# Turning the softmax weights of the hybrid layers with VectorE blocks and DMAs

## The chip, the cores and the metric

The kernel runs on one NeuronCore of a Trainium2 chip. The metric is the device time of one execution in microseconds (us), the median over several runs. Its five engines each work through a queue of their own, in order: PE (TensorE, the matrix products), DVE (VectorE), ACT (ScalarE), POOL (GpSimd) and SP (SyncE, which here issues every DMA). An instruction that must wait for a semaphore holds up all that stands behind it in its queue.

## The reference

Input is one sequence of 512 tokens, 1024 wide, in float32. One first block runs, then two hybrid layers, then a final norm. The change is in the hybrid layers, whose part that matters here is this:

```
def hybrid_layer(x, norm_gain, w_in, w_out, rel_bias, cos, sin):
    hn = rms_norm_2(x, norm_gain)
    proj = hn @ w_in                       # 1024 -> 4096
    aq, ak, av, ag, rq, rk, rv, rg = split(proj, 8 parts of 512)
    ya = chunked_rel_attention(aq, ak, av, rel_bias)   # 8 heads of 64
    yr = chunkwise_retention(rq, rk, rv, cos, sin)     # 4 heads of 128
    y = concatenate([ya * silu(ag), yr * silu(rg)])
    return x + y @ w_out
# chunked_rel_attention, one head, chunks of 64, 8 chunks to the left visible:
    scores = q k^T * dh**-0.5 + bias[distance]         # only keys up to the query's own chunk
    p = softmax(scores)
    out = p v
```

With 512 tokens every query sees all keys up to the end of its own chunk, so a head's softmax weights are the lower triangle of a 512x512 matrix, in blocks of 128.

## The kernel before, in words

All products are made in three parts of fp32r: high half times high half, and the two mixed ones. A stream of weight tiles feeds them: W.load() issues the DMA of a tile into one of NRAW raw buffers (line 277), W.split() makes its high half on ACT (line 290) and one step later its low half on DVE (line 292), and issues the load of the tile NRAW further on (line 295). Four high and four low buffers (NW) hold the split tiles. One product of a tile is 24 matmuls of 512 columns.

The order of all side work is written by hand. Each eight such matmuls count as one step (hook, line 216). A piece of side work is a Python generator: `yield n` puts its rest n steps later. So side work is spread over the product stream in fixed slots, on whichever engine it needs, in program order.

In a hybrid layer, layer_b(l), eight attention heads (head(i), line 1223) start six steps apart (line 1446), head 0 at step 13 or 12. Counted from a head's start, these are its slots in the kernel before: 0, scores of three query blocks (PE). 1, bias and row minimum (DVE). 2, last score (PE), exponentials (ACT). 3, bias of the last (DVE), load of a later head's bias (SP). 4, last exponential. 5, reciprocal (DVE) and four scalings of p (ACT, line 1274). 7, eight PE transposes into banks 5 and 6 (turn, line 1278). 8, high halves (ACT). 9, low halves (DVE). 10 to 12, the same for the two transposes that are left. 13, eight matmuls with the values (line 1305), then the copy and add to YB. Head 0 of the first hybrid layer has one step less before its transposes. The heads overlap: a head's slot 13 is the next head's slot 7. In this text AV(i) is the matmuls of head i with the values, score(i) its first scores.

Keys are made by ev_k (line 1124): they are scaled, and double_k (line 632) writes each half of 64 partitions twice, in its own place and in the other half, in high and low parts: four ACT and four DVE instructions of 64x512. After the eight heads come four retention heads, ret(i), and the output product.

The lines that the change touches otherwise: the start of the kernel, where spread_a (line 847) turns the first norm into rows and makes the FOLD matrix with six DVE instructions before the first projections are evacuated, and the placing of the buffers (lines 78 to 128).

## Time and profile before

| | us |
|---|---|
| median of 3 runs | 1222.63 (1222.36 to 1224.81) |
| the profiled execution, its own time | 1224.13 |
| span of its trace | 1222.3 |
| PE busy | 1208.9 (99%) |
| DVE busy | 842.9 (69%) |
| ACT busy | 589.4 (48%) |
| POOL busy | 287.8 (24%) |

Busy time of an engine is the time in which one of its instructions runs. The granted clock of PE is 0.8 of 2.4 GHz in the first slice of the page, and 0.9 or more in all others. Times in rows below are us from the start of the span unless they are marked ns.

### The profile page before, as it was taken

How to read it: one execution, taken by the hardware profiler on the slowest of the kernel's cores; microseconds unless marked ns; L12 is line 12 of the kernel's file. 1: busy time of each engine (PE TensorE's matmuls, PEld its weight loads, DVE VectorE, ACT ScalarE, POOL GpSimd, SP SyncE). 2: the span in 40 equal slices, each digit the busy share in tenths (PEclk: the TensorE clock that was granted, in tenths of full speed). 3: DMA queues.
4: the chain of work that ended last, by engine and by line, in shares of the span. 5: the costliest groups of instructions: out<-in, count | busy, mean ns of one | idle time of the engine just before them, and what ended most of it. 6: DMA issues, size and time to landing. Idle time of an engine off the chain costs nothing.

```text
span 1222.3 us, 15898 instructions
## 1 busy us (share of the span) xinstructions
PE 1208.9 (99%) x6061; PEld 1027.0 (84%) x6061; DVE 842.9 (69%) x1361; ACT 589.4 (48%) x1080; POOL 287.8 (24%) x299
## 2 busy tenths in 40 slices
PE   8999999999999999999999999999999999999998
PEld 7788888888888888888888879899888889899886
DVE  5889655556776577537758887767747686766746
ACT  6666432333433334224336477664435577654442
POOL 0220499912000000000006761111414211212300
PEclk8999999999999999999999999999999999999999
DMA  7422333233423433233324332222214332222211
GB/s 218 124 83 64 101 87 103 88 102 95 130 78 90 126 96 94 86 108 100 103 70 131 90 99 88 79 85 71 69 52 138 109 91 87 78 69 71 77 45 69
DMA packets 196032, 114.35 MB, mean 94 GB/s; under 512 B 3994, under 2 KB 190836, under 8 KB 195828
## 3 DMA queue, kind: packets, MB, share of 16 engines
q1 hardware_dynamic: 195956, 113.35, 31.5%
q8 instruction: 47, 0.77, 0.3%
q14 instruction: 29, 0.24, 0.1%
HBM read 111.23 MB, written 2.10 MB: 93 GB/s over the span
## 4 chain that ended last, share of the span: by engine, by line
PE 95%; DVE 3%; ACT 1%; issue 1%; DMA 1%; SPq 0%; DVEq 0%; ACTq 0%
PE ps L190 92%; PE ps L193 3%; DVE b_sets L163 1%; DMA xtm<-in_x_dram 1%; DVE wlo L163 0%; ACT b_p L160 0%; ACT whi L160 0%; DVE fold L163 0%; ACT x1l L160 0%; DVE b_pt L163 0%; DVE tmp L163 0%; DVE b_s L166 0%; SPq L196 0%; DVE nrm L166 0%; DVE b_sets L166 0%
## 5 line engine op out<-in xcount | busy, mean ns | idle before, releaser
L160 ACT ACTIVATE whi<-raw 128x1024 fp32r<-128x1024 f32 (+1 forms) x198 | 206.6, 1051 | 294.1 <-PE ps L190 293.7
L163 DVE TENSOR_TENSOR wlo<-raw,whi 128x1024 fp32r<-128x1024 f32 (+1 forms) x192 | 245.4, 1285 | 50.5 <-ACT whi L160 49.8
L190 PE MATMUL ps<-x0l,whi 128*128 128x512 f32 x1008 | 257.6, 394 | 0.0
L190 PE MATMUL ps<-x0h,whi 128*128 128x512 f32 x1008 | 255.4, 391 | 0.0
L190 PE MATMUL ps<-x0h,wlo 128*128 128x512 f32 x1008 | 254.3, 390 | 0.0
L190 PEld LDWEIGHTS ps<-x0h,whi 128*128 128x128 f32 x1008 | 188.0, 188 | 38.1
L190 PEld LDWEIGHTS ps<-x0h,wlo 128*128 128x128 f32 x1008 | 187.8, 188 | 38.3
L190 PEld LDWEIGHTS ps<-x0l,whi 128*128 128x128 f32 x1008 | 186.5, 188 | 37.4
L163 POOL TENSOR_TENSOR sums<-sums,sq 128x512 f32<-128x512 f32 x28 | 43.2, 1555 | 423.6 <-ACT sq L160 423.6
L190 PE MATMUL ps<-x1h,wlo 128*128 128x512 f32 x304 | 82.3, 389 | 0.0
L190 PE MATMUL ps<-x1h,whi 128*128 128x512 f32 x304 | 82.3, 389 | 0.0
L190 PE MATMUL ps<-x1l,whi 128*128 128x512 f32 x304 | 82.2, 389 | 0.0
L163 DVE TENSOR_TENSOR tmp<-ps,rb 128x512 f32<-128x512 f32 x54 | 37.0, 687 | 52.9 <-PE ps L190 52.7
L166 DVE SCALAR_TENSOR_TENSOR h<-ps,h 128x512 f32<-128x512 f32 x40 | 27.4, 688 | 65.2 <-PE ps L190 65.2
L160 ACT ACTIVATE b_p<-b_p,smx 128x512 f32<-128x512 f32 (+3 forms) x128 | 65.9, 553 | 8.1 <-DVE smx L177 5.2
L190 PEld LDWEIGHTS ps<-x1h,whi 128*128 128x128 f32 x304 | 57.0, 188 | 11.9
L190 PEld LDWEIGHTS ps<-x1l,whi 128*128 128x128 f32 x304 | 57.1, 188 | 11.8
L190 PEld LDWEIGHTS ps<-x1h,wlo 128*128 128x128 f32 x304 | 57.0, 188 | 11.8
L166 DVE SCALAR_TENSOR_TENSOR f_c<-f_u,cols,f_c 128x512 f32<-128x512 f32 x88 | 65.8, 749 | 1.6
L163 DVE TENSOR_TENSOR f_u<-ps,rb 128x512 f32<-128x512 f32 x44 | 30.3, 691 | 52.4 <-PE ps L190 52.3
L163 DVE TENSOR_TENSOR b_sets<-tmp,b_sets 64x512 fp32r<-64x512 f32 (+1 forms) x64 | 49.1, 768 | 15.1 <-ACT b_sets L160 13.8
L160 ACT ACTIVATE b_sets<-tmp 64x512 fp32r<-64x512 f32 (+1 forms) x64 | 40.2, 628 | 36.9 <-POOL tmp L163 34.9
(187 smaller groups left out, 1705.6 us busy)
## 6 DMA issues: line engine op xcount, KB each, us to landing
raw<-in_w_in_dram SPq DMA_DIRECT2D x98, 512.0 KB, 4.0
raw<-in_w_up_dram SPq DMA_DIRECT2D x44, 512.0 KB, 3.8
raw<-in_w_out_dram SPq DMA_DIRECT2D x24, 512.0 KB, 3.6
raw<-in_w_down_dram SPq DMA_DIRECT2D x16, 512.0 KB, 3.6
b_m<-in_rel_bias_dram SPq DMA_DIRECT2D x16, 256.0 KB, 3.3
raw<-in_w_down_dram SPq DMA_DIRECT2D x8, 384.0 KB, 3.1
xtm<-in_x_dram SPq DMA_DIRECT2D x4, 512.0 KB, 7.5
raw<-in_w_attn_branch_dram SPq DMA_DIRECT2D x8, 256.0 KB, 2.9
```

What stands on the lines that cost most here:

```text
L160: return AC.put(lambda e: e.activation(o, i, func, **kw), after, AC, 1)
L163: return on.put(lambda e: e.tensor_tensor(o, a, b, op), after, on, 1)
L166: return DV.put(lambda e: e.scalar_tensor_tensor(o, a, s, b, op0, op1), after, DV, 1)
L190: return PE.put(lambda e: e.matmul(o, l, r, start=start, stop=stop), after, PE if mark else None, 1)
L193: return PE.put(lambda e: e.transpose(o, i, ident), after, PE if mark else None, 1)
```

## The change

For each of the 16 heads (eight in each hybrid layer) the ten PE transposes go. In their slot, 7, DVE turns the weights in 32x32 blocks (six instructions, 1280 columns in all) into a buffer PD, and SP issues 16 DMAs of 32 partitions x 320 floats (40 KB each) that put the blocks in their places in PX; they wait for the last DVE instruction. In slot 10 ACT makes the high half of all 1280 columns in one instruction, which waits for all 16 DMAs. In slot 11 DVE makes the low half in one. AV stays in slot 13, but its moving operand and its output are now four pieces each, one for each 32 queries of a block, of 128, 96, 64 or 32 columns; the add to YB puts the order right.

For each of the four key tiles of a layer, double_k_by_dma makes the own half alone (two ACT and two DVE instructions), and four DMAs of 64 partitions x 512 floats (128 KB each) copy it into the other half. The DMA of the high parts waits for ACT, that of the low parts for DVE. The scores of heads wait for these DMAs.

Room for PD and PX (10 KB in each partition) comes from the raw weight buffers, 3 in place of 5, from the mask, which moves into a region that the first block alone uses, and from the second bias buffer, which moves into X1L. So the first load into that buffer in a layer waits for the last product before it. FOLD is made later, after the projections of the first block.

```diff
--- before.py
+++ after.py
@@ -75,7 +75,7 @@
             top[0] += (4 * floats + 31) // 32 * 32
             return at(name, floats, off, dt)
 
-        NRAW, NW = 5, 4
+        NRAW, NW = 3, 4
         RAW = sb("raw", NRAW * 1024)
         WHI = sb("whi", NW * 1024, F32R)
         WLO = sb("wlo", NW * 1024, F32R)
@@ -86,7 +86,7 @@
         X1H, X1L = sb("x1h", 4096, F32R), sb("x1l", 4096, F32R)
         XTM = at("xtm", 4096, x1_off)
         RB = sb("rb", 512)
-        CA = sb("ca", 456)
+        CA = sb("ca", 200)
         ones_off = top[0]
         ONESR = sb("ones", 128, F32R)
         FOLD = at("fold", 128, ones_off)
@@ -105,14 +105,15 @@
                 off += (4 * floats + 31) // 32 * 32
             return got
 
-        XMH, XML, PA, PTA, ZC, ROWS = pool_plan("a_", [
+        XMH, XML, PA, PTA, ZC, ROWS, RX, MASK = pool_plan("a_", [
             ("xmh", 4096, F32R), ("xml", 4096, F32R), ("p", 1024, F32), ("pt", 2048, F32R),
-            ("zc", 514 * 2 + 512 * 2, F32), ("rows", 384, F32)])
-        RX = at("rx", 512, (pool_off + 4 * (4096 * 2 + 1024 + 2048 + 514 * 2 + 512 * 2 + 384) + 31) // 32 * 32)
+            ("zc", 514 * 2 + 512 * 2, F32), ("rows", 384, F32),
+            ("rx", 512, F32), ("mask", 256, F32)])
         _, UB, CB = pool_plan("f_", [("sums", 2048, F32), ("u", 4 * 514, F32), ("c", 4 * 512, F32)])
-        SETS, PB, PTB, S2, MB = pool_plan("b_", [
+        SETS, PB, PTB, S2, MB, PD, PX = pool_plan("b_", [
             ("sets", 8192, F32R), ("p", 2560, F32), ("pt", 2560, F32R),
-            ("s2", 1024, F32), ("m", 1024, F32)])
+            ("s2", 1024, F32), ("m", 512, F32), ("pd", 1280, F32), ("px", 1280, F32)])
+        MB2 = at("mb2", 512, x1_off + 4 * (4096 + 4 * 512))
 
 
 
...
@@ -491,7 +494,8 @@
         t_rows = dma(rows[2], fc[0:128, :], d_rows)
         W.load()
         t_snk = dma(COLS[:, 264:272], bass.AP(tensor=sinks.tensor, offset=sinks.offset, ap=[[0, 128], [1, 8]]), d_snk)
-        t_c = dma(CA[:, 128:451], const_a[:, 128:451], d_c)
+        dma(MASKN, const_a[:, 128:384], d_c)
+        t_c = dma(CA[:, 128:195], const_a[:, 384:451], d_c)
         for _ in range(NRAW - 3):
             W.load()
         act(COLS[:, 280:281], ONES[:, 0:1], after=t_ones)
@@ -650,6 +654,25 @@
                 toks[e].append(tl)
             return toks
 
+        def double_k_by_dma(khs, kls, t, after, free, done):
+
+            own = []
+            for e in range(2):
+                r, o = rows_of(e)
+                own.append(act(khs[e][r, :], t[r, :], after=[after, free]))
+            yield 1
+            for e in range(2):
+                r, o = rows_of(e)
+                dma(f32(khs[e][o, :]), f32(khs[e][r, :]), done, after=[own[e], free])
+            lows = []
+            for e in range(2):
+                r, o = rows_of(e)
+                lows.append(tt(kls[e][r, :], t[r, :], f32(khs[e][r, :]), ALU.subtract, after=[after, own[e], free]))
+            for e in range(2):
+                r, o = rows_of(e)
+                tok = dma(f32(kls[e][o, :]), f32(kls[e][r, :]), done, after=lows[e])
+            return [own, lows, [tok]], own + lows
+
         def stack_q(qs, t, bias, after, free):
 
             toks = []
@@ -846,10 +869,6 @@
 
         def spread_a():
             rb["rb"] = spread_rows(RB[:, :], va["diag"], 7)
-            t = tt(FOLD[:, 0:32], IDENT[:, 0:32], IDENT[:, 32:64], ALU.add, after=rb["rb"])
-            for i in (64, 96):
-                t = tt(FOLD[:, 0:32], FOLD[:, 0:32], IDENT[:, i:i + 32], ALU.add, after=t)
-            va["fold"] = [copy(FOLD[:, i:i + 32], FOLD[:, 0:32], after=t) for i in (32, 64, 96)]
 
         banks = Banks([3, 5, 1, 2, 0])
         first_tiles([evac_k, evac_v, evac_q(0)], [norm_a, lambda: None, spread_a], [(0, tok0)])
@@ -899,6 +918,11 @@
         def rotary_sines():
             c = act(ROT[:, 0:512], ROT[:, 0:512], ACT.Sin, scale=TWOPI, after=[rot["turns"], t_c])
             rot["tok"] = [c, act(ROT[:, 512:1024], ROT[:, 512:1024], ACT.Sin, scale=SGN, after=rot["turns"])]
+
+        t = tt(FOLD[:, 0:32], IDENT[:, 0:32], IDENT[:, 32:64], ALU.add, after=rb["rb"])
+        for i in (64, 96):
+            t = tt(FOLD[:, 0:32], FOLD[:, 0:32], IDENT[:, i:i + 32], ALU.add, after=t)
+        va["fold"] = [copy(FOLD[:, i:i + 32], FOLD[:, 0:32], after=t) for i in (32, 64, 96)]
 
         rotary_turns()
 
@@ -1080,9 +1104,11 @@
         pbs = Slots([PB[:, 0:1280], PB[:, 1280:2560]])
         ptbs = Slots([PTB[:, :]])
         ybs = Slots([YB[:, :]])
-        ms = Slots([MB[:, 0:512], MB[:, 512:1024]])
+        ms = Slots([MB[:, :], MB2[:, :]])
         PO_T = [0, 128, 384, 768]
         PT_K = [0, 512, 1024, 896]
+        AT_K = [0, 4, 7, 9]
+        pd_free, px_free = [[]], [[]]
 
         def layer_b(l):
             nonlocal banks
@@ -1100,6 +1126,7 @@
                 a = ts(o[:, 0:448], o[:, 0:448], -1.0, None, ALU.mult, after=t, on=PO)
                 bias_of[i] = k, o, [a, tt(o[:, 448:512], AHEAD, o[:, 448:512], ALU.subtract, after=[t, t_c], on=PO)]
 
+            ms.free[1] = [ms.free[1], W.done[W.n_take - 1]]
             load_bias(0)
             load_bias(1)
 
@@ -1126,8 +1153,8 @@
                     k, t, a = scaled(bank, tok)
                     yield 1
                     v = views(s)
-                    tok_k[s] = yield from double_k(v["kh"], v["kl"], t, None, a, qk_free[s % 2])
-                    T.free[k] = tok_k[s]
+                    toks, T.free[k] = yield from double_k_by_dma(v["kh"], v["kl"], t, a, qk_free[s % 2], d_k[s % 2])
+                    tok_k[s] = [toks, toks]
                 return go
 
             def ev_q(s):
@@ -1265,6 +1292,8 @@
                 tm[1] = biased(1, tp1)
                 bank_free[3] = [tm[1]]
                 ms.free[km] = [tm[1]]
+                if km == 1:
+                    slot_free[4].append(tm[1])
                 if i < 6:
                     load_bias(i + 2)
                 yield 1
@@ -1275,39 +1304,32 @@
                 smx.free[ks] = [t_p[3]]
                 yield rest
 
-                def turn(kt, bank, c0, free):
-                    for t in range(kt, 4):
-                        tp = tr(PS[bank][:, c0 + 128 * (t - kt):c0 + 128 * (t - kt) + 128],
-                                p[t][:, 128 * kt:128 * kt + 128], IDENT, after=[t_p[t], free], mark=t == 3)
-                    return tp
-
-                t0 = turn(0, 5, 0, claim(5))
-                free = claim(6)
-                turn(1, 6, 0, free)
-                t1 = turn(3, 6, 384, free)
-                yield 1
+                pd = PD[:, :].rearrange("p (i x c) -> p x i c", i=4, c=32)
+                for t, k0, k1, x0, x1, dx in ((0, 0, 1, 0, 1, 1), (1, 0, 2, 1, 5, 3), (2, 0, 2, 2, 6, 3), (2, 2, 3, 7, 8, 1),
+                                              (3, 0, 2, 3, 7, 3), (3, 2, 4, 8, 10, 1)):
+                    tb = blocks(pd[:, x0:x1:dx, :, :], p[t][:, 128 * k0:128 * k1].rearrange("p (k i c) -> p k i c", i=4, c=32),
+                                after=[t_p[t], pd_free[0]])
+                pbs.free[kp] = [tb]
+                for j in range(4):
+                    for d in range(4):
+                        t_px = dma(PX[32 * d:32 * d + 32, 320 * j:320 * j + 320], PD[32 * j:32 * j + 32, 320 * d:320 * d + 320],
+                                   d_px, after=[tb, px_free[0]])
+                pd_free[0] = [t_px]
+                yield 3
                 _, pt, tfree = ptbs.take()
                 hi, lo = pt[:, 0:1280], pt[:, 1280:2560]
-                th = [act(hi[:, 512 * j:512 * j + 512], PS[5 + j][:, :], after=[(t0, t1)[j], tfree]) for j in range(2)]
-                yield 1
-                tl = [tt(lo[:, 512 * j:512 * j + 512], PS[5 + j][:, :], f32(hi[:, 512 * j:512 * j + 512]),
-                         ALU.subtract, after=[th[j], tfree]) for j in range(2)]
-                bank_free[5], bank_free[6] = [tl[0]], [tl[1]]
-                yield 1
-                tp = turn(2, 5, 0, claim(5))
-                pbs.free[kp] = [tp]
-                yield 1
-                th.append(act(hi[:, 1024:1280], PS[5][:, 0:256], after=tp))
-                yield 1
-                tl.append(tt(lo[:, 1024:1280], PS[5][:, 0:256], f32(hi[:, 1024:1280]), ALU.subtract, after=th[2]))
-                bank_free[5] = [tl[2]]
-                yield 1
+                th = act(hi, PX[:, :], after=[t_px, tfree])
+                yield 1
+                tl = tt(lo, PX[:, :], f32(hi), ALU.subtract, after=[t_px, th, tfree])
+                px_free[0] = [th, tl]
+                yield 2
                 o, free = PS[7], claim(7)
+                by_q = lambda a, x0, x1: a.rearrange("p (q x) -> p q x", q=4)[:, :, 32 * x0:32 * x1]
                 for kt in range(4):
-                    n = 512 - 128 * kt
                     vk = v_at(s // 2, kt)[:, s % 2, 128 * e:128 * e + 128]
-                    mm(o[:, 128 * kt:512], vk, hi[:, PT_K[kt]:PT_K[kt] + n], kt == 0, False, after=[tok_v[s // 2], th, free])
-                    tp = mm(o[:, 128 * kt:512], vk, lo[:, PT_K[kt]:PT_K[kt] + n], False, kt == 3, after=tl, mark=kt == 3)
+                    x0, x1 = AT_K[kt], AT_K[kt] + 4 - kt
+                    mm(by_q(o[:, :], kt, 4), vk, by_q(hi, x0, x1), kt == 0, False, after=[tok_v[s // 2], th, free])
+                    tp = mm(by_q(o[:, :], kt, 4), vk, by_q(lo, x0, x1), False, kt == 3, after=tl, mark=kt == 3)
                 ptbs.free[0] = [tp]
                 if e == 1:
                     v_read[s] = [tp]
@@ -1323,7 +1345,9 @@
                     y_half[s] = yfree
                 else:
                     yfree = y_half[s]
-                t2 = tt(backwards(YB[r, :]), tiles(o[r, :]), tiles(t[r, :]), ALU.add, after=[t1, yfree])
+                q4 = lambda a: a.rearrange("p (q t c) -> p q t c", q=4, t=4)
+                y = YB[r, :].rearrange("p (t q c) -> p q t c", q=4, t=4)[:, ::-1, :, ::-1]
+                t2 = tt(y, q4(o[r, :]), q4(t[r, :]), ALU.add, after=[t1, yfree])
                 bank_free[7] = [t2]
                 T.free[k] = [t2]
                 if e == 1:
```

## Rows read from the trace of the kernel before

**Rows 1.** The page, busy time of each engine: us, share, instructions.
```profile
PE 1208.9 (99%) x6061; PEld 1027.0 (84%) x6061; DVE 842.9 (69%) x1361; ACT 589.4 (48%) x1080; POOL 287.8 (24%) x299
```

**Rows 2.** Windows: stretch, its us, busy us (count) by engine, clock, DMA share, GB/s.
```profile
682.00:717.70 35.70, 34.14 (x204) 29.93 (x204) 32.54 (x59) 22.54 (x47) 30.51 (x19) 1.00 0.32 95
717.70:813.00 95.30, 95.30 (x573) 84.73 (x573) 70.71 (x141) 68.18 (x144) 16.28 (x14) 1.00 0.28 81
```

**Rows 3.** The chain that ended last, in order of time: start, us, what.
```profile
33.31 2.12 DVE fold L163
...
36.25 0.60 DVE tmp L163
...
724.25 0.87 PE ps L193 x8
...
732.13 0.22 PE ps L193 x2
```

**Rows 4.** Timeline of PE: start, us, engine, line, what, count, idle before and releaser.
```profile
40.64 0.66 PE L193 MATMUL ps<-ca,tmp 128*128 128x128 f32 x4 [1.26 <-ACT tmp L160]
...
717.24 0.44 PE L193 MATMUL ps<-ca,b_p 128*128 128x128 f32 x2 [1.23 <-DVE b_pt L163]
...
827.32 1.38 PE L190 MATMUL ps<-b_pt,x1h 128*128 128x512 f32 x8
...
977.69 1.20 PE L190 MATMUL ps<-b_sets 128*128 128x512 f32 x6
...
994.02 1.04 PE L193 MATMUL ps<-ca,b_p 128*128 128x128 f32 x8
...
1008.75 1.04 PE L193 MATMUL ps<-ca,b_p 128*128 128x128 f32 x8
...
1098.11 1.38 PE L190 MATMUL ps<-b_pt,x1h 128*128 128x512 f32 x8
```

**Rows 5.** Groups on PE, shapes apart: busy us, mean ns, idle before.
```profile
L193 PE MATMUL ps<-ca,b_p 128*128 128x128 f32 x192 | 27.5, 272 | 1.2 <-DVE b_pt L163 1.2
```

**Rows 6.** Groups on DVE, shapes apart: busy us, mean ns, idle before.
```profile
L163 DVE TENSOR_TENSOR wlo<-raw,whi 128x1024 fp32r<-128x1024 f32 x184 | 237.9, 1299 | 50.2 <-ACT whi L160 49.5
L163 DVE TENSOR_TENSOR b_sets<-tmp,b_sets 64x512 fp32r<-64x512 f32 x48 | 38.2, 795 | 1.2
L163 DVE TENSOR_TENSOR b_pt<-ps,b_pt 128x512 fp32r<-128x512 f32 x32 | 20.6, 685 | 10.7 <-ACT b_pt L160 10.6
L181 DVE STREAM_TRANSPOSE rb<-nrm 128x512 f32<-128x512 f32 x4 | 2.7, 701 | 0.1
L181 DVE STREAM_TRANSPOSE sq<-sums 128x1024 f32<-128x1024 f32 x1 | 1.2, 1233 | 0.0
```

**Rows 7.** Groups on ACT, shapes apart.
```profile
L160 ACT ACTIVATE whi<-raw 128x1024 fp32r<-128x1024 f32 x190 | 200.0, 1059 | 282.0 <-PE ps L190 281.6
L160 ACT ACTIVATE b_pt<-ps 128x512 fp32r<-128x512 f32 x32 | 17.3, 593 | 27.6 <-PE ps L190 27.6
```

**Rows 8.** Timeline of ACT: the four scalings of one head.
```profile
1004.81 1.93 ACT L160 ACTIVATE b_p<-b_p,smx 128x128 f32<-128x128 f32 x4
```

**Rows 9.** Timeline of the DMA issues on SP: start, us.
```profile
10.82 0.32 SPq L196 DMA_DIRECT2D a_rows<-in_norm_gain_dram  x1
11.17 0.38 SPq L196 DMA_DIRECT2D a_rows<-in_conv_w_dram  x1
...
111.87 0.37 SPq L196 DMA_DIRECT2D raw<-in_w_attn_branch_dram  x1
112.28 0.51 SPq L196 DMA_DIRECT2D raw<-in_w_conv_branch_dram  x1
```

**Rows 10.** DMA issues: target, count, KB each, median us from issue to landing.
```profile
raw<-in_w_in_dram SPq DMA_DIRECT2D x98, 512.0 KB, 4.0
b_m<-in_rel_bias_dram SPq DMA_DIRECT2D x16, 256.0 KB, 3.3
raw<-in_w_attn_branch_dram SPq DMA_DIRECT2D x8, 256.0 KB, 2.9
raw<-in_w_conv_branch_dram SPq DMA_DIRECT2D x8, 256.0 KB, 3.3
ca<-in_const_a_dram SPq DMA_DIRECT2D x1, 64.0 KB, 1.9
```

**Rows 11.** Timeline of DVE and ACT near the kernel's start.
```profile
28.78 3.49 DVE L163 TENSOR_TENSOR wlo<-raw,whi 128x1024 fp32r<-128x1024 f32 x3
31.73 1.06 ACT L160 ACTIVATE whi<-raw 128x1024 fp32r<-128x1024 f32 x1 [4.39 <-PE ps L190]
32.70 0.58 ACT L160 ACTIVATE rb<-ps 128x512 f32<-128x512 f32 x1
```

**Rows 12.** Timeline of DVE in the first hybrid layer.
```profile
710.80 5.31 DVE L163 TENSOR_TENSOR b_sets<-tmp,b_sets 64x512 fp32r<-64x512 f32 x4
```

More of the change, by code:

```diff
@@ L140, in block_then_hybrid_layers @@
         IDENT = CA[:, 0:128]
-        MASKN = CA[:, 128:384]
-        INVF = CA[:, 384:385]
-        SGN = CA[:, 385:386]
-        TWOPI = CA[:, 386:387]
-        AHEAD = CA[:, 387:451]
+        MASKN = MASK[:, :]
+        INVF = CA[:, 128:129]
+        SGN = CA[:, 129:130]
+        TWOPI = CA[:, 130:131]
+        AHEAD = CA[:, 131:195]
         TURN = [part * 2.0 ** (-12 * i - 12) for i, part in enumerate((0x28B, 0xE60, 0xDB9, 0x391, 0x054))]
@@ L423, in block_then_hybrid_layers @@
         d_gain = Counter(sem("s_gain"))
+        d_px = Counter(sem("s_px"))
+        d_k = [Counter(sem(f"s_k{i}")) for i in range(2)]
         d_out = Counter(sem("s_out"))
```

## The prediction, made before the changed kernel was run

> **What bounds the kernel now.** I read the busy times first: PE is busy 99% of the span, the next engine, DVE, 69% [rows 1]. So only work taken off PE, or PE's few waits, can shorten the kernel. The windows of the stage with the heads come second: PE never pauses there, while DVE has 70.7 of 95.3 us of work and ACT 68.2 [rows 2]. The reader is to see that both have room, but not much: 10.9 and 10.5 us in each head's period of 14.74 us (994.02 to 1008.75, from one head's transposes to the next one's) [rows 4]. Third, the chain in order of time prices the transposes: eight take 0.87 us and two 0.22, so 1.09 a head; their mean of 272 ns is that of overlapping matmuls [rows 3, 5]. Fourth, PE's waits that the change touches: 1.26 us near 40 us, and 1.23 us at 717 us before head 0's last two transposes [rows 4].
>
> **What PE saves.** 16 heads x 1.09 = 17.4 us, plus up to 1.2 us at 717. The columns of AV stay 1280 twice. That they come in pieces of 32 to 128 is not in the trace, whose moving operands are whole. From zero to the transposes' price again (doubling AV's 1.1 us at every head, 17 us) is possible; I take zero, since the nearest rows, 128-column transposes and 512-column matmuls alike, pay for columns.
>
> **What the other engines get, for each head.** DVE: six block turns. 512 columns took 0.70 us and 1024 took 1.23 [rows 6], so about 0.16 each and 1.04 ns a column: 2.2 us with overlapped starts. One low half of 1280 columns instead of three costs 1.5 in place of 1.8 [rows 6]. Half keys save two 64x512 instructions of 0.7 to 0.8 us a tile [rows 6], three tiles in the stage. DVE goes to about 12.2 us of a period that would be 13.65. ACT gets lighter: one high half of 1.3 us for three of 1.6, and two copies fewer a key tile [rows 7].
>
> SP: 16 issues. Small issues start 0.35 us apart (10.82 to 11.17), large ones 0.41 [rows 9]; I take 0.36, so the last starts 5.4 us after the first. Landing: the nearest in size, 64 KB, took 1.9 us from issue; the bias loads took 3.3 [rows 10]. I take 1.9, as these are 40 KB and read no DRAM. Turn-around from the last block to ACT's start is then 7.4 us with hand-offs. Its bounds are 15 x 0.32 + 1.9 = 6.7 and 15 x 0.41 + 3.3 = 9.5.
>
> The page "DMA: Bandwidth & Descriptors" of the Trainium skill (section "Anatomy of one DMA") gives about 2.0 us plus bytes/436e3 for one DMA: 2.1 us for 40 KB. By it the turn-around would be 0.2 us longer and the time some 3 us more than mine. No row here shows a transfer between two places in SBUF.
>
> **Does it fit?** The slots leave three steps, 6.8 us, from the blocks to the high half, and three more to AV. A single head would fit: 7.4 + 1.3 + 1.5 = 10.2 us, against some 13 before PE reaches AV. But the heads are coupled through ACT and DVE, which work in order. ACT stands at high(i) until the 16 DMAs of head i have landed. Behind it in ACT's queue are the last exponential and the four scalings of head i+1, and behind low(i) in DVE's queue its reciprocal and its blocks. So each head's DMAs start only after the DMAs of the one before have been used. One round:
>
> - high half 1.3, low half 1.5, reciprocal 0.2;
> - DVE's work in slots 11 and 12 ahead of the blocks: two low parts of a projection 1.5, an evacuation 0.65;
> - blocks 2.2, issues 5.4, landing 1.9, hand-offs 0.1.
>
> That is 14.8 us. Where a value tile or a gate is in those slots it is 14.2 (then the scalings' 1.93 us [rows 8] set it); where head 3's X1 low half or the first retention keys fall in, 15.4 to 15.7. By the order of the projections the seven rounds are 2 x 14.8, 3 x 14.2, 15.7 and 15.4: 103.3 us. Without a limit, seven periods would be 7 x 13.65 = 95.6; before they are 103.2. So the loop gives back nearly all that PE saves, except what the slots hold as slack.
>
> **The sum.** Second hybrid layer: score(1) starts at 977.69 [rows 4]. Evacuation 0.65, blocks 2.2, turn-around 7.4: high(0) at 988.0. Seven rounds and 2.8 more: low(7) is ready at 1094.1, where AV(7) was at 1098.11 [rows 4]: 4.0 us earlier, of 8.7 that the transposes alone would give. First hybrid layer: before, head 0's blocks would come after the next head's bias on DVE, beside POOL's work, about 711.3; high(0) at 718.7, low(7) at 824.8, AV(7) was at 827.32 [rows 4]: 2.5 us, the wait at 717 included. DVE gains room there: four key instructions at 710.80 took 5.31 us [rows 12] and become two. After AV(7) PE is the bound again, so both gains stay.
>
> Start: without FOLD the first evacuation moves 2.9 us forward (33.31 to 36.25) [rows 3]. But with 3 raw buffers, tile 6's load waits for tile 3's low half, done near 30.0 us, lands 4.0 later [rows 10], and its ACT split, now at 31.73, stands ahead of the row factors at 32.70 [rows 11]. Those move to about 35.0, the evacuation to 35.7. Gain 0.6 us. Elsewhere a load is issued about three tiles (16 us) before its split and needs 4 us; 5.8 us of DMA issues ahead of it on SP still fit. The extra wait of the second bias load on SP is for the matmul that the next split waits for anyway: nothing.
>
> The copies of keys cost SP four issues a tile, and a wait on ACT and one on DVE, behind which stand weight loads with that same slack. I see one place where scores would wait: the fourth keys' DMAs follow head 4's sixteen, so score(6) could wait some 3 us; AV(5) is later than that by the loop, so I count nothing. Uncovered it would be up to 3 us a layer.
>
> Total: 4.0 + 2.5 + 0.6 = 7.1 us. The profiled execution takes 1224.13 us: 1217.0. The median of the runs lies 1.5 us below that execution, so **1215.5 us**.
>
> **Rivals.** Each 0.1 us in a round is worth 14 x 0.1 = 1.4 us.
>
> A: the rounds fit, with issues of 0.32 us and DVE work that runs ahead; all transposes are gained. 17.4 + 1.2 + 0.6 = 19.2: 1203.4. For it: PE has no wait in these stages, DVE and ACT idle a quarter of them [rows 2]. Against: a round must lose 1.1 us.
>
> B, slower: the landing is that of the bias loads or the issues are slower, so that the turn-around is 8.8 (15 x 0.38 + 3.1). Rounds grow by 1.4, 19.6 us, to 1235. It decides from a turn-around of 7.9 (a round of 15.3), and DVE at 80% or more adds to it wherever an instruction waits for ACT. Against: the 64 KB row.
>
> C: the 16 transfers don't overlap their fixed part. At 1.9 us each a turn-around is 30 us, a round 38, the time near 1530. The two loads of branch weights, issued 0.41 us apart at 111.87 and 112.28, land in 2.9 and 3.3 us [rows 9, 10], so they do overlap. The same page of the Trainium skill, "Rules for kernel authors", says of two transfers to disjoint partition halves that they serialize; by it the time would be C's. The trace speaks against it for the fixed part.
>
> D: the loop is as I say, but short prefetch or keys that land late take the gain: 3 us a layer for keys and 1 at the start, 1222.
>
> **Chances.** Forecast (1209 to 1220) 0.42; A 0.19; B 0.27; C 0.01; D 0.11. What a measurement can tell from no change is 0.2%, 2.4 us. Faster: forecast and A, 0.61. Within: most of D and the edges of the forecast and B, 0.12. Slower: 0.27. The range for 8 in 10 reaches into A and B: 1204 to 1234.
>
> **What would show it.** PE should wait about 1 us at most AVs from the second or third head on, released by the low half on DVE; ACT should wait for px DMAs at each high half, by 1 us or more; the distance from one head's high half to the next should be 14 to 16 us; the issues of the sixteen should start 0.36 us apart. If ACT never waits for them, A is right. If landing is over 2.5 us, B is. If a stall of PE has weights or keys as its releaser, my account of the raw buffers or of the copies is wrong. If AV's eight matmuls take more than 1.5 us, their pieces cost.

## The result: slower by 4.9%

The changed kernel takes 1283.26 us (median of 4 runs, 1281.37 to 1284.47), the kernel before 1222.64 beside it: 1.049 times, 95% interval 1.0472 to 1.0509. Forecast were 1215.5 us in a range of 1204 to 1234.

The page of the profile after, busy times and the chain that ended last:

```profile
PE 1214.4 (95%) x5901; PEld 1024.7 (80%) x5901; DVE 853.8 (67%) x1409; ACT 576.0 (45%) x1032; POOL 284.7 (22%) x299
...
PE 75%; SPq 10%; DVE 6%; DMA 3%; ACT 3%; issue 3%; DVEq 0%; ACTq 0%
...
b_px<-b_pd SPq DMA_DIRECT2D x256, 40.0 KB, 1.9
...
b_sets<-b_sets SPq DMA_DIRECT2D x32, 128.0 KB, 4.5
```

The reader is to see three things against [rows 1]. PE is now idle for 67.9 us of a span of 1282.3, where it was idle 13.4. It is busy 5.5 us longer, though its 160 transposes of weights (17.4 us by the forecast's count) are gone. And a tenth of the chain is SP's queue, which means issuing DMAs: it moves no data and computes nothing.

The windows of the two stages with the heads (us; busy us and count of PE, PEld, DVE, ACT, POOL; granted clock, DMA share, GB/s), and below them two short stretches of the second stage:

```profile
717.70:854.00 136.30, 108.96 (x562) 93.20 (x562) 84.88 (x171) 69.19 (x134) 16.56 (x16) 0.90 0.41 111
992.00:1154.00 162.00, 133.97 (x683) 114.15 (x682) 101.13 (x207) 83.28 (x163) 15.52 (x15) 0.92 0.40 109
1026.50:1030.50 4.00, 4.00 (x11) 3.42 (x12) 3.17 (x10) 0.29 (x1) 1.59 (x2) 0.50 0.47 117
1030.50:1034.50 4.00, 4.00 (x19) 3.31 (x19) 1.43 (x3) 1.27 (x4) 0.00 (x0) 0.86 0.26 68
```

Before, PE was busy in all of such a window at clock 1.00 [rows 2]. Now 27 and 28 us of each are idle, and the clock is granted at 0.90 and 0.92.

The DMA issues on SP, in the second hybrid layer (start, us, what, count):

```profile
1009.02 10.06 SPq L197 DMA_DIRECT2D b_px<-b_pd  x16
1019.12 0.59 SPq L197 DMA_DIRECT2D raw<-in_w_in_dram  x1
1019.75 2.51 SPq L197 DMA_DIRECT2D b_sets<-b_sets  x4
1022.31 0.58 SPq L197 DMA_DIRECT2D mb<-in_rel_bias_dram  x1
1022.94 0.46 SPq L197 DMA_DIRECT2D raw<-in_w_in_dram  x1
1027.27 10.73 SPq L197 DMA_DIRECT2D b_px<-b_pd  x16
```

Sixteen issues take 10.06 us, so one starts every 0.63 us. The second sixteen take 10.73, since one of their issues took 1.25 us. The weight load and the keys' copies stand behind them in the queue, at the same pace. The groups by line (min/median/max ns) show where this differs from an issue that stands alone; the last line is from the kernel before:

```profile
L197 SPq DMA_DIRECT2D b_px<-b_pd x256: 507/591/1717, 709.1 to 1149.4; - x128
...
L197 SPq DMA_DIRECT2D raw<-in_w_in_dram x98: 367/368/1480, 2.1 to 1183.9; - x98
...
L197 SPq DMA_DIRECT2D raw<-in_w_conv_branch_dram x8: 508/508/578, 126.9 to 232.5; - x8
```
```profile
L196 SPq DMA_DIRECT2D b_m<-in_rel_bias_dram x16: 340/341/581, 668.5 to 1043.4; - x16
```

The usual weight load, which stands alone, takes 0.37 us; the branch load that always comes second of two, 0.51. The load of a bias takes 0.34 alone and 0.58 in the two places where it stands right behind a weight load (668.54 and 940.62 in the kernel before), so the place in the queue has a price. So has the kind of transfer: the first of each sixteen, with no issue right ahead of it, already takes 0.51 to 0.57 us, and the others 0.59.

ACT and DVE through one round (in brackets the idle time before, and its releaser):

```profile
1039.35 1.27 ACT L161 ACTIVATE b_pt<-b_px 128x1280 fp32r<-128x1280 f32 x1 [1.01 <-DMA b_px<-b_pd]
...
1042.34 1.93 ACT L161 ACTIVATE b_p<-b_p,smx 128x128 f32<-128x128 f32 x4
...
1058.40 1.27 ACT L161 ACTIVATE b_pt<-b_px 128x1280 fp32r<-128x1280 f32 x1 [6.61 <-DMA b_px<-b_pd]
```
```profile
1040.73 1.49 DVE L164 TENSOR_TENSOR b_pt<-b_px,b_pt 128x1280 fp32r<-128x1280 f32 x1 [0.71 <-ACT b_pt L161]
1042.14 0.17 DVE L1302 RECIPROCAL smx<-smx 128x4 f32<-128x4 f32 x1
1042.22 1.37 DVE L164 TENSOR_TENSOR b_sets<-tmp,b_sets 64x512 fp32r<-64x512 f32 x2
1043.63 0.69 DVE L167 SCALAR_TENSOR_TENSOR tmp<-ps,rb 128x512 f32<-128x512 f32 x1
1044.24 1.80 DVE L182 STREAM_TRANSPOSE b_pd<-b_p 128x128 f32<-128x128 f32 x6
```

This is the forecast's loop, in its order: high half 1039.35, low half, reciprocal, DVE's work of the slots, scalings beside it, blocks until 1046.04, issues, landing, and the next high half at 1058.40. That round is 19.05 us. Over seven rounds the mean is 18.7 in both layers (720.54 to 851.48 and 1020.42 to 1151.32).

PE meanwhile (timeline):

```profile
1026.47 2.26 PE L191 MATMUL ps<-b_sets 128*128 128x512 f32 x6 [7.70 <-DVE b_pd L182]
1028.53 3.44 PE L191 MATMUL ps<-x0h,whi 128*128 128x512 f32 x8
...
1045.43 1.38 PE L191 MATMUL ps<-b_pt,b_sets 128*128 128x512 f32 x8
...
1061.32 1.26 PE L191 MATMUL ps<-b_pt,b_sets 128*128 128x512 f32 x7 [1.09 <-DVE b_pt L164]
```

PE waits once for 7.70 us ahead of score(2), and three more times a like amount (8.94 at 726.53, 8.71 at 799.99, 8.91 at 1100.68), and 1.2 to 3.1 us at seven of the sixteen AVs (the waits for the high and the low half sum to 8.9 and 8.0 us). The row names DVE, but what came last before it is a landing: the fourth of the keys' copies was issued at 1021.67 and landed at 1026.33, 0.14 us before score(2). The other three long waits end in the same way. After the long wait PE runs for 4 us at the lower of its two levels (granted clock 0.50, which is 1.2 GHz): the eight matmuls at 1028.53 take 3.44 us, where such eight take 1.99 at 1037.02.

### The profile page after: what moved, and what is told of

It reads as the page before. It is cut to its first block, busy times and chain, and to the rows that moved or that the text cites. A ratio compares the mean times of both kernels' runs of the same rounds, so it can differ in the third digit from the quotient of the medians.

```text
span 1282.3 us, 15878 instructions
## 1 busy us (share of the span) xinstructions
PE 1214.4 (95%) x5901; PEld 1024.7 (80%) x5901; DVE 853.8 (67%) x1409; ACT 576.0 (45%) x1032; POOL 284.7 (22%) x299
## 4 chain that ended last, share of the span: by engine, by line
PE 75%; SPq 10%; DVE 6%; DMA 3%; ACT 3%; issue 3%; DVEq 0%; ACTq 0%
PE ps L191 74%; SPq L197 10%; DMA b_px<-b_pd 2%; DVE b_pd L182 2%; ACT b_pt L161 1%; PE ps L194 1%; DVE b_pt L164 1%; DVE tmp L164 1%; DMA xtm<-in_x_dram 1%; DVE b_sets L164 1%; ACT b_p L161 1%; DVE wlo L164 0%; ACT whi L161 0%; DMA raw<-in_w_in_dram 0%; DVE x1l L164 0%
## 5 line engine op out<-in xcount | busy, mean ns | idle before, releaser
L191 PE MATMUL ps<-x0h,whi 128*128 128x512 f32 x1008 | 261.1, 398 | 0.0
L191 PEld LDWEIGHTS ps<-x0h,whi 128*128 128x128 f32 x1008 | 192.5, 193 | 39.4
L191 PEld LDWEIGHTS ps<-x0l,whi 128*128 128x128 f32 x1008 | 190.7, 192 | 38.9
L191 PE MATMUL ps<-b_sets 128*128 128x512 f32 (+2 forms) x224 | 48.0, 345 | 36.2 <-DVE b_pd L182 16.6
L164 DVE TENSOR_TENSOR b_pt<-b_px,b_pt 128x1280 fp32r<-128x1280 f32 x16 | 26.1, 1629 | 78.9 <-ACT b_pt L161 78.9
L191 PEld LDWEIGHTS ps<-b_sets 128*128 128x128 f32 x224 | 40.1, 205 | 44.7 <-ACT b_p L161 18.4
```

The lines of the kernel that those rows point to most:

```text
L164: return on.put(lambda e: e.tensor_tensor(o, a, b, op), after, on, 1)
L191: return PE.put(lambda e: e.matmul(o, l, r, start=start, stop=stop), after, PE if mark else None, 1)
```

## The experiments

Two theories stood at the start. **Pace:** the rounds are as forecast, but each of the 16 issues costs 0.63 us on SP, and this alone sets the turn-around. **Keys:** what counts is the four long waits at the scores of head pairs, where the keys' copies come late behind the sixteen on SP. A third, that the transfers' shape or bytes are slow, was kept for the size tests. Times are medians beside runs of the kernel before on the same chip (1223.24 to 1223.44). Each of the first kernels is the changed kernel with the edit shown.

**Keys copied by engines again.**

```diff
-                    toks, T.free[k] = yield from double_k_by_dma(v["kh"], v["kl"], t, a, qk_free[s % 2], d_k[s % 2])
-                    tok_k[s] = [toks, toks]
+                    tok_k[s] = yield from double_k(v["kh"], v["kl"], t, None, a, qk_free[s % 2])
+                    T.free[k] = tok_k[s]
```


> The changed kernel with the keys' second copies made by ACT and DVE again; the rest of the change stays. Theory 1 (pace of issues): the sixteen issues of a head start 0.63 us apart in place of my 0.36, so a round from one head's high half to the next one's takes about 18.7 us in place of 14.8, and that alone sets the stage; taking the keys' DMAs away only removes 4 x 0.6 us of issues per two heads and adds 1.5 us of DVE work, so rounds stay at 18 to 19 us and the time at 1270 to 1282 us. Theory 2 (keys): the two waits of 8 to 9 us a layer before scores, 34 us in all, with the lower clock behind them, are the loss; without them the time falls to about 1235 us.

1284.62 us, 1.0498 (1.0483 to 1.0514): nothing is won. PE's waits of this kernel (us in total, times, longest):

```profile
PE ps L191 <- ACT b_p L161: 24.7, 4, 7.3
PE ps L191 <- ACT b_pt L161: 11.5, 7, 2.0
PE ps L191 <- DVE b_pt L164: 8.0, 8, 1.1
```

The four long waits stay, shorter (24.7 us in all, where they were 34.3), and now name ACT. Score(2) starts at 1025.41. The high and low parts that it reads are made by ACT and DVE at 1023.27 and 1024.58, behind the high half of 1021.60: the scores wait for what the coupled rounds delay, with or without keys' DMAs. The rounds are as long as before (18.9 and 18.7 us in the mean of each layer). Keys is out as the cause of the loss, though it is what ends these four waits in the changed kernel.

**Transposes on PE again**, keys by DMA as in the change; and **both undone**, which leaves only the layout (3 raw buffers, FOLD built later, the mask apart). The edit puts the old body of the head (turn(), three high and three low parts, AV on whole tiles, the old order of YB) in the place of the blocks, and for the second kernel also the edit above.

```diff
-                pd = PD[:, :].rearrange("p (i x c) -> p x i c", i=4, c=32)
...
-                yield 3
+                def turn(kt, bank, c0, free):
...
-                    mm(by_q(o[:, :], kt, 4), vk, by_q(hi, x0, x1), kt == 0, False, after=[tok_v[s // 2], th, free])
+                    mm(o[:, 128 * kt:512], vk, hi[:, PT_K[kt]:PT_K[kt] + n], kt == 0, False, after=[tok_v[s // 2], th, free])
```


> The changed kernel with the ten PE transposes of each head again; keys' copies by DMA, 3 raw buffers and the new places stay. Theory 1: nothing of the size of the loss is left, since SP is free and a key tile's four issues take 2.5 us; 1219 to 1226 us, no wait of scores over 1 us. Theory 2 in its strong form (the copies' own latency is too long for their slot): waits of several us before score(2) and score(6) stay, 1235 us or more.

> The changed kernel with both parts undone: 3 raw buffers in place of 5, the mask and the second bias buffer in their new places, and the later FOLD are all that is left of the change. Theory 1 and 2: 1221 to 1224 us, the same as before within 0.2%, with the row factors of the first norm about 2 us later and FOLD's 2.9 us off the path. Theory 3 (short prefetch): waits for raw weights show on PE and the time is 1230 us or more.

1221.01 us, 0.9979 (0.9969 to 0.9988), and 1223.05 us, 0.9996 (0.9987 to 1.0006). So the layout is worth nothing, the keys' DMAs 2 us to the better when no burst stands ahead of them, and the whole loss is in the turning of the weights. The wait of 1.2 us at 717 [rows 4] stays in the second kernel and is gone from the first.

**Four wide transfers in place of the sixteen** (same bytes; the blocks aren't exchanged between partition groups, so that part of the transposition is left out).

```diff
-                    for d in range(4):
-                        t_px = dma(PX[32 * d:32 * d + 32, 320 * j:320 * j + 320], PD[32 * j:32 * j + 32, 320 * d:320 * d + 320],
-                                   d_px, after=[tb, px_free[0]])
+                    t_px = dma(PX[:, 320 * j:320 * j + 320], PD[:, 320 * j:320 * j + 320], d_px, after=[tb, px_free[0]])
```


> The changed kernel with 4 DMAs of 128 partitions x 320 floats in place of 16 of 32 x 320: the same bytes from PD to PX, but the blocks are not exchanged between partition groups, so this part of the computation is left out. Theory 1: issues take 4 x 0.6 us, the turn-around falls from 12 to 4.5 us, a round would be 12 us and PE is the bound again; waits of scores vanish as SP is free early; 1203 to 1208 us. If the landing of 640 KB or the other steps of the round set the pace, and not the number of issues: 1225 us or more.

1207.91 us, 0.9872 (0.9857 to 0.9887). SP, and the landing from the page:

```profile
1013.01 2.40 SPq L197 DMA_DIRECT2D b_px<-b_pd  x4
...
b_px<-b_pd SPq DMA_DIRECT2D x64, 160.0 KB, 2.2
```

Four transfers of 160 KB are issued at the same 0.60 us each, and land in 2.2 us. The turn-around is some 7 us shorter, and PE has lost nearly all its waits (1193.3 us busy, span 1207.5).

**Sixteen thin transfers** (the same part left out): as many issues as the change, but 128 partitions by 80 columns.

```diff
-                for j in range(4):
-                    for d in range(4):
-                        t_px = dma(PX[32 * d:32 * d + 32, 320 * j:320 * j + 320], PD[32 * j:32 * j + 32, 320 * d:320 * d + 320],
-                                   d_px, after=[tb, px_free[0]])
+                for j in range(16):
+                    t_px = dma(PX[:, 80 * j:80 * j + 80], PD[:, 80 * j:80 * j + 80], d_px, after=[tb, px_free[0]])
```


> The changed kernel with 16 DMAs of 128 partitions x 80 floats in place of 16 of 32 x 320: the same number and the same bytes, but the blocks are not exchanged between partition groups, so this part of the computation is left out. It is the control for four_wide (1207.9). Theory 1 (the number of issues counts, not their shape): pace 0.63 us, 1278 to 1290 us. Rival (transfers of 32 partitions are slow, wide ones are not): 1225 us or less.

1284.13 us, 1.0494 (1.0477 to 1.0512): the changed kernel's time. Its group of issues:

```profile
L197 SPq DMA_DIRECT2D b_px<-b_pd x256: 464/601/1856, 708.7 to 1151.7; - x128
```

The number of issues decides, not their partitions, columns or bytes.

**Twelve issues.** On top of the keys by engines, the four transfers that stay on their own partitions become copies on POOL (the lines that keep POOL's copies in order are left out here).

```diff
+                own_px = (PO, PO.n)
+                for d in range(4):
+                    own_px = copy(PX[32 * d:32 * d + 32, 320 * d:320 * d + 320], PD[32 * d:32 * d + 32, 320 * d:320 * d + 320],
+                                  after=[own_px, tb, px_free[0]], on=PO)
...
+                        if d != j:
```


> keys_on_engines with 12 DMAs a head instead of 16: the four blocks that stay in their partition group are copied by POOL. Theory 1 (issues at 0.63 us, in a round that couples the heads): the turn-around falls by 4 x 0.63 = 2.5 us, the round from about 18.4 to 15.9 us, against a PE period of 13.65; of the 77 us between keys_on_engines (1284.6) and four_wide (1207.9) about 36 stay: 1240 to 1250 us. Rival (a fixed latency or the bytes set the round, and the number of issues is beside the point): 1275 us or more.

1249.81 us, 1.0218 (1.0203 to 1.0234). Four issues fewer at 0.63 us in 16 heads are 40 us, and 35 us came back: the pace gives the sign and most of the size.

**Half of the issues on another queue**, on ACT's and then on POOL's:

```diff
+                        if j % 2:
+                            t_py = AC.put(lambda e, to=to, src=src: e.dma_start(to, src), [tb, px_free[0]], d_py, 16)
+                        else:
+                            t_px = dma(to, src, d_px, after=[tb, px_free[0]])
+                t_px = [t_px, t_py]
```


> keys_on_engines with 8 of the 16 DMAs issued by ACT and 8 by SP. Theory 1a (each queue has its own pace of 0.63 us): both halves are issued in 5 us, the turn-around falls from 12 to 7 us; ACT pays 5 us of issues a head, so a round is about 15 us: 1222 to 1240 us. Theory 1b (the pace is that of something both queues share): 16 issues still take 10 us, the two queues' issues are each about 1.2 us apart, and ACT is held longer: 1284 us or more.

> keys_on_engines with 8 of the 16 DMAs issued by POOL and 8 by SP. Theory 1a (own pace of each queue): SP's eight take 5 us; if POOL's take no longer the round is about 13.5 us and the time 1205 to 1215 us; if a POOL issue takes 1 us, the turn-around is 10 us and the time about 1255 us. Theory 1b (shared): 1284 us or more.

1260.02 us, 1.0303 (1.0288 to 1.0318), and 1238.34 us, 1.0119 (1.0097 to 1.014). With ACT, the two queues run side by side, eight issues each:

```profile
1015.12 5.27 SPq L197 DMA_DIRECT2D b_px<-b_pd  x8
...
1015.12 5.59 ACTq L1318 DMA_DIRECT2D b_px<-b_pd  x8
```

So each queue has its own pace, and the issues are done in half the time. The Trainium skill ("DMA: Bandwidth & Descriptors", section "Rules for kernel authors") says that spreading DMAs over queues only saves the sequencer's issue time. The trace agrees: landing stays at 1.9 to 2.0 us, and issue time is here the very thing that bounds.

But ACT pays for its eight: it can neither evacuate nor split while it waits for the blocks and issues (16 such stretches, 97.5 us in all). PE's largest wait in that kernel is for what DVE makes behind ACT:

```profile
PE ps L191 <- DVE b_sets L164: 27.1, 4, 8.4
```

POOL has room, and 22 us more come back. What stays is the coupling: ACT still stands 50.5 us at the high halves, where it stood 94.0 with all sixteen on SP.

**Decoupled.** The loop itself is cut: the high half moves three slots later (slot 13 of the head; AV to slot 16), behind the next head's scalings in ACT's queue and its blocks in DVE's. The DMAs write back into the weights' own buffer, of which there are three, so nothing waits for px. Keys by engines, all sixteen on SP.

```diff
-        pbs = Slots([PB[:, 0:1280], PB[:, 1280:2560]])
+        pbs = Slots([PB[:, 0:1280], PB[:, 1280:2560], PX[:, :]])
...
-                        t_px = dma(PX[32 * d:32 * d + 32, 320 * j:320 * j + 320], PD[32 * j:32 * j + 32, 320 * d:320 * d + 320],
-                                   d_px, after=[tb, px_free[0]])
+                        t_px = dma(pb[32 * d:32 * d + 32, 320 * j:320 * j + 320], PD[32 * j:32 * j + 32, 320 * d:320 * d + 320],
+                                   d_px, after=tb)
...
-                yield 3
+                yield 6 if i < 7 else 4
...
-                th = act(hi, PX[:, :], after=[t_px, tfree])
+                th = act(hi, pb, after=[t_px, tfree])
```


> keys_on_engines with the high half moved from slot 10 to 13, the low half to 14 and AV to 16 (head 7: 11, 12, 14), and the DMAs writing back into the head's own buffer of p, of which there are three. All 16 DMAs stay and compute the whole reference. Theory 1 with coupling (the loss comes from ACT standing at the high half ahead of the next head's softmax): SP needs 11 us of a 13.65 us period, ACT never waits long, PE is the bound: 1203 to 1212 us. Rival (SP's load itself, weight loads behind ten microseconds of issues, or DVE at over 90%): PE waits for raw weights or evacuations, 1225 us or more.

1224.26 us, 1.001 (1.0 to 1.002). Against 1284.62 with the same issues at the same pace, 60 us are back. The slow issues hurt because the next head's DMAs waited, through ACT's and DVE's order, for this head's. That cause is shown. The edit also gives the DMAs other buffers, but in the changed kernel PX was free at 1042.22 and the blocks ended only at 1046.04, so it was not the buffer that the DMAs waited for. The gain does not come, though. PE's idle time is 25.9 us, 12.5 more than before the change, in small pieces: for low halves 4.7 us, for the biases 4.6, and for h and yb 4.5, in places behind head 7, whose high half still waits for its DMAs (10.04 and 8.59 us on ACT). PE and DVE at one of the waits for a bias:

```profile
797.21 0.51 PE L191 MATMUL ps<-b_sets 128*128 128x256 f32 x2 [1.85 <-DVE smx L178]
```
```profile
793.32 1.41 DVE L164 TENSOR_TENSOR tmp<-ps,rs 64x512 f32<-64x512 f32 x2
794.76 1.81 DVE L182 STREAM_TRANSPOSE b_pd<-b_p 128x128 f32<-128x128 f32 x6
796.49 0.66 DVE L178 CUSTOM_DVE_ANT_0 b_p<-ps,mb 128x512 f32<-128x512 f32 x1
```

The blocks stand right ahead of the next head's biases, whose banks PE needs, and 1.8 us more in that place is what PE waits.

**Decoupled, eight of the sixteen on POOL, keys by DMA.** DVE gets rid of the key copies and SP of half the burst.

```diff
+                    toks, T.free[k] = yield from double_k_by_dma(v["kh"], v["kl"], t, a, qk_free[s % 2], d_k[s % 2])
...
+                        if j % 2:
+                            t_py = PO.put(lambda e, to=to, src=src: e.dma_start(to, src), tb, d_py, 16)
```


> decoupled (1224.3) with 8 of the 16 DMAs on POOL's queue and the keys' copies by DMA again. If what is left there is SP's load and DVE's (both get relief: SP 5 us a head, DVE 1.5 us a key tile), PE's 15 us of waits fall by half: 1208 to 1216 us. If it is the order on DVE (the blocks stand ahead of the next head's bias, which frees the bank that PE's last score needs), the waits released by smx stay and the time is 1215 us or more.

1220.58 us, 0.9979 (0.997 to 0.9989): 2.7 us less than before, which is small but clear of the noise, and equal to the kernel that only changes the keys. PE's waits in it:

```profile
PE ps L191 <- DMA b_sets<-b_sets: 6.7, 2, 4.0
PE ps L194 <- DMA xtm<-in_x_dram: 3.3, 1, 3.3
PE ps L191 <- ACT x1h L161: 2.9, 1, 2.9
```

PE is busy 1195.3 us, 13.6 less than before, and the span is only 4.6 shorter: waits of 1 to 4 us at single places took 9. The wait for xtm was there before; new are those for the keys' copies (4.0 and 2.7) and for x1h. The waits for the biases have shrunk from 4.6 us to 0.5, with the blocks still ahead of the biases. So this order was not what held PE here: the time is that of the second case of the expectation, the waits are those of the first.

**The same with the blocks one slot later**, so that the biases go first:

```diff
-            def head(i, rest=2):
+            def head(i, rest=3):
...
-                yield 6 if i < 7 else 4
+                yield 5 if i < 7 else 3
```


> dec_pool_keys with the blocks one slot later (8 in place of 7), so behind the next head's bias on DVE; the high half stays in slot 13, which the split leaves room for. If the order on DVE is what holds PE in decoupled, its waits for smx vanish: 1203 to 1210 us. If not: as dec_pool_keys.

1225.91 us, 1.0027 (1.0015 to 1.0039): a miss. The 0.5 us that was left of the waits for the biases is gone, but the last head's transfers are again too late for its high half, which waited 3.4 us at most in the kernel above:

```profile
822.62 1.27 ACT L161 ACTIVATE b_pt<-b_p 128x1280 fp32r<-128x1280 f32 x1 [10.16 <-DMA b_p<-b_pd]
```

ACT stands there 10 us in each layer, as in the kernel with all sixteen on SP, and what it does behind it (h, the next projection) reaches PE late: 4.9 us for h, 3.0 for yb.

**Decoupled, twelve on SP and four copies on POOL, keys by DMA** (the edit of "Twelve issues" in place of the split):

```diff
-                        if j % 2:
-                            t_py = PO.put(lambda e, to=to, src=src: e.dma_start(to, src), tb, d_py, 16)
-                        else:
-                            t_px = dma(to, src, d_px, after=tb)
+                        if d != j:
```


> decoupled with 12 DMAs, all on SP, the four diagonal blocks copied by POOL, and the keys' copies by DMA. Issues take 7.5 us a head; SP carries about 10.5 us of a 13.65 us period. The second key tile's copies stand behind head 0's twelve, so score(2) may wait 2 to 5 us a layer. 1212 to 1222 us.

1234.33 us, 1.0088 (1.0073 to 1.0103): a miss too. SP, and PE's longest wait:

```profile
709.49 7.55 SPq L198 DMA_DIRECT2D b_p<-b_pd  x12
717.08 0.58 SPq L198 DMA_DIRECT2D raw<-in_w_in_dram  x1
717.71 2.51 SPq L198 DMA_DIRECT2D b_sets<-b_sets  x4
```
```profile
725.15 2.26 PE L192 MATMUL ps<-b_sets 128*128 128x512 f32 x6 [7.21 <-DMA b_sets<-b_sets]
```

Here the keys' copies do cost: four waits of 4.4 to 7.2 us and one of 0.3, 23.3 us in all. Once the rounds no longer bind, 7.6 us of burst ahead of the keys bind in their place. With eight of the issues on POOL and blocks in slot 7, the same row is 5.01 us and the wait at that score 4.00.

## Why the prediction was wrong

**The step that failed** is "16 issues ... I take 0.36, so the last starts 5.4 us after the first". Measured: 0.63 apart, so that the last starts 9.4 us after the first, and 9.8 in the mean of the sixteen bursts. The bounds, 0.32 to 0.41, failed too. They were read from the small row loads at the kernel's start and from a pair of weight loads, and a burst of sixteen was not in the trace. [Rows 9] held a sign: the second of the pair at 111.87 took 0.51 us against 0.37. I read only the distance between the two starts (0.41), which is the price of the first, and passed over the duration of the second; the bias load of 0.34 alone and 0.58 behind a weight load says the same. But the burst is not all of it: the first of each sixteen took 0.51 to 0.57 with no issue right ahead of it, and the small row loads go five in a row at 0.29 to 0.38 each (10.48 to 11.94 in the kernel before). So the nearest rows were too cheap in kind as well as in place, and what sets the price of one issue stays open.

By the prediction's own rules this one term gives the result. 15 x (0.63 - 0.36) = 4.05 us at each of 16 turn-arounds is 64.8 us; 1215.5 + 64.8 = 1280.3, and 1283.3 was measured. The rounds say the same: 18.7 measured less 14.76 forecast is 3.9 us. That the sum comes so close is in part luck. The turn-arounds were 4.35 us longer than forecast (mean of the sixteen 11.75, against 7.4), 0.3 more than the pace explains, because seven of the 256 issues took 1.0 to 1.7 us; the rest of a round was 0.4 shorter, which the shorter blocks account for.

**Right:** the loop through ACT and DVE, its order and its coupling; landing 1.9 us; the high half 1.27 (1.3 forecast), the low 1.49 (1.5), the scalings 1.93. The blocks took 1.80 in twelve heads, 0.4 less than forecast, and 2.29 in four. AV in pieces costs nothing: eight matmuls 1.38 us, as before [rows 4]. The transfers overlap (each lands 1.9 us after its issue, and the next issues start 0.63 us apart, so about three are in flight), so rival C is out. (Its time is also summed too low: 14 rounds longer by 23.2 us give 1540, not 1530, before the first turn-arounds are counted.) At the start, raw buffers do what was said (the weight load that waits for a buffer enters the chain at 29.73 and lands 3.86 us later), and the gain of 0.6 us is too small to be told from none: the layout alone measured 0.9996.

**Rival B** was this case with too low a price. Its mechanism (a turn-around over 7.9 us costs 1.4 us for each 0.1) held, but I priced it at 8.8, inside bounds that ended at the slowest values seen (9.5); measured turn-arounds are 11.4, 12.1 and 12.4 us in the second layer's first rounds (blocks done at 1008.99, 1027.24 and 1046.04, high halves at 1020.42, 1039.35 and 1058.40). The chance of 0.27 for slower was also too low for a sum that lay 0.5 us in a turn-around from the turning point and contained a term seen only alone.

**Left out of the sum:** the clock. PE was busy 5.5 us longer without its 17.4 us of transposes, so its other work took 22.9 us more; the windows with granted clock 0.90 and 0.92 are where it went. Over the whole trace PE was busy for 45.3 us in stretches with granted clock 0.50, before for 5.3. By an estimate from these two numbers, 40 us more at half the rate cost 20 of the 22.9. Together with 54.5 us of added idle time that is the 60.0 us of the span. It isn't a second cause on top of the 64.8: while the loop sets the end, slower matmuls use up time in which PE would have waited. The kernel with keys by engines agrees: PE is idle 60.8 us there, 7.1 less, and busy 6.4 longer, 56.4 us of it at 0.50, and the rounds and the time are the same. No run held the clock apart, though.

**Keys:** I said up to 3 us at score(6), covered by the loop. Score(2) was left out: its keys' copies too stand behind a burst of sixteen. The copies land 4.5 us after their issue, and by the forecast's own sign (a stall of PE that keys release) its account of the copies was wrong. Two scores in each layer wait 8 to 9 us for them, but it is cover that counts: taking the keys' DMAs out changed nothing (1284.62). In the kernels without the loop the same term came out uncovered, at 23.3 us with twelve issues ahead. So "hidden" was right for this kernel and for none of its repairs.

**Where the gain went.** Even with the issues made cheap (four wide) the kernel is at 1207.9, near rival A's 1203.4; and the versions that compute the whole reference stop at 1220.6. None of them merged the sixteen issues into fewer transfers. So of some 17 us, waits at single places took most: low halves and blocks ahead of biases in one kernel, keys behind bursts in three, the last head's short distance to its AV in two. Whether another order of slots removes all of them at once stays open; the two places tried for the blocks did not.

## What to carry to other kernels

Before small DMAs replace an engine's work, count their issues and price them by an issue of the same kind in a burst, not by a lone issue of another kind; look for how long the second of two neighbours takes, and give the term a bound above the slowest value seen. Then ask which in-order engine stands at the landing, and whether the next round's issues depend on what is queued behind it: cutting that dependence was worth 60 us here, and handing half of the issues to POOL's queue 46. A queue that carries the burst also carries loads and copies with their own due times.

## What the runs showed of the hardware

- Issues on SP: a weight load takes 0.37 us alone and 0.59 behind a burst, a bias load 0.34 alone and 0.58 behind a weight load; transfers within SBUF take 0.51 to 0.57 as the first of sixteen, then 0.59 with 0.04 of gap; the same pace for 32x320, 128x80 and 128x320 elements and for the keys' 64x512 (four in 2.51 us). The Trainium skill ("DMA: Bandwidth & Descriptors", section "Anatomy of one DMA", which treats the GpSimd path) puts the sequencer's dispatch at about 50 ns and the generation of descriptors as small and variable. On SP's queue, which that section does not treat, the trace shows 0.63 us each in a burst, and on POOL's own 0.50 each (128 issues of 496 to 704 ns); the measurement decides. The forecast's 2.1 us for a transfer was from the same section, and 1.9 was measured on SP's queue.
- SP and ACT issue eight each in 5.27 and 5.59 us at the same time.
- A transfer from PD to PX lands 1.9 us after its issue for 40 KB and 2.2 us for 160 KB, with about three in flight at a time. The keys' copies, also within SBUF and of 128 KB, land after 4.5 us (3.8 to 5.1). They stand near loads of weights and biases in the queue; whether that or their shape makes them slower, no run separates.
- From the end of a wait of 7.7 us, PE's granted clock was 0.50 for 4 us, 0.86 for the next 4, and eight matmuls took 3.44 us in place of 1.99.
